# The first up-projection step of six feed-forward passes, made in token halves

## The chip, the cores and the metric

The kernel runs as one launch on one core of a Trainium2 chip. The metric is the device time of that launch in microseconds, the median of the runs. Five engines work side by side and meet only through semaphores: TensorE (PE, with its weight loads listed as PEld), VectorE (DVE), ScalarE (ACT), GpSimd (POOL) and SyncE (SP). Transfers run on DMA queues.

## The reference, cut to what matters

Two blocks follow each other over one sequence of 256 tokens with 1024 features, each block with two layers. Every layer has a feed-forward pass (hidden width 2816), a mix of three branches with gates, and a second feed-forward pass:

```python
def swiglu(x, w_in, w_out):
    a, b = jnp.split(x @ w_in, 2, axis=-1)
    return (jax.nn.silu(a) * b) @ w_out

# first block, each of 2 layers
x = x + 0.5 * swiglu(rmsnorm(x, ffn1_norm[l]), w_ffn1_in[l], w_ffn1_out[l])
...                                       # the mix
x = x + 0.5 * swiglu(rmsnorm(x, ffn2_norm[l]), w_ffn2_in[l], w_ffn2_out[l])
# second block, each of 2 layers
x = _layer_norm(DN_ALPHA * x + 0.5 * _swiglu(x, ffn1_w1[l], ffn1_w2[l]), ln1_g[l], ln1_b[l])
...                                       # the mix, and its layer norm
x = _layer_norm(DN_ALPHA * x + 0.5 * _swiglu(x, ffn2_w1[l], ffn2_w2[l]), ln3_g[l], ln3_b[l])
```

That makes eight feed-forward passes. All data are float32.

## The kernel before, in words

**Tiling.** Tokens are 2 tiles of 128 (`TT`), features 8 tiles of 128 (`KD`), the hidden width 22 tiles (`FT`). The residual stream `x` and its normalised copy `xn` lie with tokens on the partitions. A product wants features on the partitions, so PE transposes: `turn` (L403 to L412) makes four 128x128 transposes (the instruction is L410) into a PSUM bank `T0` or `T1`; `turn_x` (L414) does so for token tile 0, features 0 to 3 in `T0` and 4 to 7 in `T1`, and then the same for token tile 1. Each filled bank is then read twice: ACT rounds it into `xT_upper` (L1519, `uppers`), and DVE writes the remainder to `xT_rest` (L1010, `rests`) and so releases the bank.

**Products in two parts.** Weights and activations are each held as a float32r upper part and a float32r rest. `product` makes three matmuls for one product: upper by upper, upper by rest, rest by upper. All matmuls are recorded under L361.

**The stream of weights.** The weights come as pieces of 128x1024 float32, 220 for each layer. SP loads a piece into one of four places of `ring`; ACT rounds it into `upper` (L1519), POOL subtracts to `rest` (L896) and thereby empties the ring place, so that SP may load it again. `upper` and `rest` have four places too; a place is free when PE has made the last matmul on it, which `mm` signals with the next matmul that carries no other signal (`free()` puts the piece on a list, `state["free"]`). ACT and POOL work ahead of PE by at most four pieces.

**A feed-forward pass.** `ffn` (L480) makes for each hidden tile j an `up(j)` (L488) and, one tile behind, a `down(j - 1)` (L500). `up(j)` takes two pieces (v = 0, 1, the two halves of the first weight matrix) and fills one PSUM bank `A0` or `A1`: for each piece 8 feature tiles of 3 matmuls with 256 moving columns (both token tiles), 48 matmuls in all. ACT then makes the silu of the first half, DVE multiplies by the second and splits into `hT`. `down(j)` takes one piece: 4 output banks `Y0` to `Y3` of 3 matmuls with 512 columns.

**Order before a pass.** In six of the eight passes `turn_x` stands directly ahead of the pass: `ffn(0)` and `ffn(1)` of the first block and `ffn(1)` of the second, in two layers each. The pass starts with `wait_xT` (L421), which waits until DVE has read both banks of token tile 1. The two other passes (`ffn(0)` of the second block) find `xT` already turned. Every engine runs its own program in the order written; there is no planner at run time.

Of the kernel before, what the change touches and what calls it, by code (L numbers as in the profile page):

```python
# [23 lines left out]
ALL = slice(None)  # L24

P = 128
# [121 lines left out]
def emit(nc, a, book):  # L148
# [4 lines left out]
    with ExitStack() as ctx:  # L153
# [202 lines left out]
        def _(pe):  # L356
# [31 lines left out]
            def cut(parts, *index):  # L388
                return tuple(p[index] for p in parts)
# [21 lines left out]
                    at_col += P  # L411
                i.then_inc(*filled(label))  # L412

            def turn_x(src, label, ready):  # L414
                for tt in range(TT):
                    pe.wait_ge(*ready(tt))
                    for h in range(2):
                        turn(f"T{h}", label + (tt, h),
                             [src[:, tt, (4 * h + q) * P:(4 * h + q + 1) * P] for q in range(4)])

            def wait_xT(label):  # L421
                for h in range(2):
                    pe.wait_ge(*taken(label + (1, h)))
# [53 lines left out]
                            also(k, cut(s, ALL, q))  # L477
                    free()

            def ffn(f, xlabel):  # L480

                if xlabel is None:
                    for h in range(2):
                        pe.wait_ge(*sig[f"T{h} read"].value(0))
                else:
                    wait_xT(xlabel)

                def up(j):  # L488
                    lab = ("ab", f, j)
                    out = fill(pe, f"A{j % 2}", lab)  # L490
                    for v in range(2):
                        s = shaped(piece(), PIECE, "p (k c) -> p k c", k=KD)
                        for k in range(KD):
                            product(out[:, v * S:(v + 1) * S], cut(s, ALL, k), cut(xT, ALL, k),
                                    k == 0, k == KD - 1, filled(lab) if v == 1 and k == KD - 1 else None)
                        free()

                ys = []

                def down(j):  # L500
                    s = piece()
                    pe.wait_ge(*sig["hidden"].after((f, j)))
                    if j == 0:
                        ys.extend(fill(pe, f"Y{b}", ("y", f, b)) for b in range(4))
                    for t in range(TT):
                        for n in range(2):
                            product(ys[2 * t + n], cut(hT, ALL, j % 2, slice(t * P, (t + 1) * P)),
                                    cut(s, ALL, slice(n * 512, (n + 1) * 512)),
                                    j == 0, j == FT - 1, filled(("y", f, 2 * t + n)) if j == FT - 1 else None)
                    free()  # L510

                for j in range(FT):
                    up(j)
                    if j:
                        down(j - 1)
                down(FT - 1)
                state["A"] = 0
# [82 lines left out]
            with region(pe, BLOCK1):  # L600
                state["piece"] = 0
                assert not state["free"]
                turn_x(xn, ("norm", 0), lambda tt: sig["scaled"].after((0, tt)))
                ffn(0, ("norm", 0))

                pe.wait_ge(*sig["memory scaled"].after(0))
                by_features("mk", 2, rhs=(memTg,))
# [111 lines left out]
                          lambda h, kt: VX[:, kt, h * P:(h + 1) * P], P, False, between=turn_both)  # L719
                turn_o("mem", lambda qt: taken(("o", "mem", 0, qt)))  # L720
                merge()
                turn_x(xn, ("norm", 2), lambda tt: sig["scaled"].after((2, tt)))
                ffn(1, ("norm", 2))
                leave_last()

            with region(pe, BETWEEN):
# [15 lines left out]
            with region(pe, BLOCK2):  # L742
                state["piece"] = 0
                assert not state["free"]
                ffn(0, None)
                turn_x(x, ("norm", 0), lambda tt: sig["x normed"].after((0, tt)))
                wait_xT(("norm", 0))
                by_features("qa", 2)
# [82 lines left out]
                    free()  # L831
                turn_o("fox", lambda qt: taken(("o", "fox", 1, qt)))
                merge()
                turn_x(x, ("norm", 1), lambda tt: sig["x normed"].after((1, tt)))
                ffn(1, ("norm", 1))
                leave_last()
                turn_x(x, ("norm", 2), lambda tt: sig["x normed"].after((2, tt)))

# [1133 lines left out]
```

## Time and profile before

| | us |
|---|---|
| median of 3 runs | 3139.74 (3139.7 to 3140.13) |
| profiled execution, its own time | 3141.49 |
| span of that execution, first to last instruction | 3139.8 |
| PE busy | 2877.2 (92%) |
| POOL busy | 2067.8 (66%) |
| ACT busy | 1232.5 (39%) |
| DVE busy | 946.9 (30%) |
| mean granted TensorE clock | 0.950 of full |

Busy times are of one profiled execution. A matmul's record lasts longer than the step from its start to the next one's start, since matmuls overlap; what a run of n matmuls costs is read from starts, or as (length of the merged row, less one record) / (n - 1). The granted clock is 1.00 at 2.4 GHz and 0.50 at 1.2 GHz.

### The profile page before, as it was taken

Reading aid. Unit: us, or ns where it says so; the run is one execution under the profiler, and the core shown is the slowest. Engines: PE = TensorE matmul, PEld = TensorE weight load, DVE = VectorE, ACT = ScalarE, POOL = GpSimd, SP = SyncE. Lnnn points to the kernel's source line nnn. Section 1 sums busy time; section 2 is a strip of 40 time slices with the busy share of each in tenths; the row PEclk is TensorE's granted clock in tenths of the full one; section 3 lists DMA queues with packets and bytes.
Section 4 is the critical chain, followed back from the end, with each engine's and each line's share of the span. In section 5 each row is a group of like instructions: output and inputs, shape, how many; then the busy total and the mean of one; then the engine's idle time right before and its main releaser. Section 6 shows DMA issues by size and latency. Waiting matters only on the chain.

```text
span 3139.8 us, 55072 instructions
## 1 busy us (share of the span) xinstructions
PE 2877.2 (92%) x19786; PEld 2676.7 (85%) x19786; DVE 946.9 (30%) x1601; ACT 1232.5 (39%) x1522; POOL 2067.8 (66%) x905
## 2 busy tenths in 40 slices
PE   5999979899899988899899899888989989988898
PEld 4997778899798868889889899888989989988897
DVE  2111274311211146521111222752121122375212
ACT  3433434344442443344344343334443434333444
POOL 4875454788685734578768774347877867425787
PEclk8999989999899999999899998999999999999999
DMA  5555433555554532355545454235555544413554
GB/s 204 188 176 169 140 108 100 178 187 188 172 187 155 189 121 95 127 182 188 170 159 186 151 167 148 68 108 174 187 176 172 184 150 157 154 61 111 178 188 155
DMA packets 131939, 491.31 MB, mean 156 GB/s; under 512 B 14656, under 2 KB 14656, under 8 KB 129632
## 3 DMA queue, kind: packets, MB, share of 16 engines
q1 hardware_dynamic: 128256, 467.10, 45.3%
q0 software_dynamic: 3424, 20.71, 1.9%
q8 instruction: 167, 2.74, 0.4%
q14 instruction: 92, 0.75, 0.1%
HBM read 485.63 MB, written 2.13 MB: 155 GB/s over the span
## 4 chain that ended last, share of the span: by engine, by line
PE 38%; issue 27%; POOL 26%; DVE 6%; ACT 1%; POOLq 1%; DMA 0%; DVEq 0%; ACTq 0%; SPq 0%
POOL rest L896 26%; PE psA L361 23%; PE psY L361 13%; PE psT L410 2%; DVE st L1086 1%; ACT Sc L1519 1%; POOLq L893 1%; DVE xT_rest L1010 0%; DVE PT L1318 0%; ACT xT_upper L1519 0%; DVE Sc L1091 0%; DVE Sc L1081 0%; DVE xT_upper L1169 0%; DVE arena L1165 0%; DMA cst<-in_consts 0%
## 5 line engine op out<-in xcount | busy, mean ns | idle before, releaser
L896 POOL TENSOR_TENSOR rest<-ring,upper 128x1024 fp32r<-128x1024 f32 (+1 forms) x836 | 2025.8, 2429 | 919.6 <-ACT upper L1519 902.6
L1519 ACT ACTIVATE upper<-ring 128x1024 fp32r<-128x1024 f32 (+1 forms) x836 | 877.0, 1050 | 1048.3 <-PE psA L361 833.4
L361 PE MATMUL psA<-xT_upper,upper 128*128 128x256 f32 x3456 | 987.3, 286 | 16.8 <-DVE xT_rest L1010 12.7
L361 PE MATMUL psA<-xT_rest,upper 128*128 128x256 f32 x3456 | 985.8, 285 | 0.0
L361 PE MATMUL psA<-xT_upper,rest 128*128 128x256 f32 x3456 | 985.6, 285 | 0.0
L361 PEld LDWEIGHTS psA<-xT_upper,upper 128*128 128x128 f32 x3456 | 671.3, 194 | 28.0 <-issue 19.8
L361 PEld LDWEIGHTS psA<-xT_rest,upper 128*128 128x128 f32 x3456 | 671.2, 194 | 6.2
L361 PEld LDWEIGHTS psA<-xT_upper,rest 128*128 128x128 f32 x3456 | 670.9, 194 | 0.0
L1066 DVE TENSOR_TENSOR sil<-sil,psA 128x256 f32<-128x256 f32 x176 | 74.1, 421 | 1257.6 <-ACT sil L1519 1257.6
L361 PE MATMUL psY<-upper,hT_upper 128*128 128x512 f32 x704 | 276.0, 392 | 0.0
L361 PE MATMUL psY<-rest,hT_upper 128*128 128x512 f32 x704 | 275.9, 392 | 0.0
L361 PE MATMUL psY<-upper,hT_rest 128*128 128x512 f32 x704 | 273.9, 389 | 0.0
L361 PE MATMUL psY<-xT_upper,upper 128*128 128x256 f32 (+1 forms) x784 | 236.4, 302 | 6.4 <-POOL rest L896 6.3
L361 PE MATMUL psY<-xT_rest,upper 128*128 128x256 f32 (+1 forms) x784 | 228.4, 291 | 0.0
L361 PE MATMUL psY<-xT_upper,rest 128*128 128x256 f32 (+1 forms) x784 | 227.9, 291 | 0.0
L1519 ACT ACTIVATE sil<-psA 128x256 f32<-128x256 f32 x176 | 67.7, 385 | 295.6 <-PE psA L361 295.6
L361 PEld LDWEIGHTS psY<-xT_upper,upper 128*128 128x128 f32 (+1 forms) x784 | 155.9, 199 | 7.1 <-POOL rest L896 6.7
L361 PEld LDWEIGHTS psY<-xT_rest,upper 128*128 128x128 f32 (+1 forms) x784 | 156.1, 199 | 1.8
L361 PEld LDWEIGHTS psY<-upper,hT_rest 128*128 128x128 f32 x704 | 132.2, 188 | 28.9
L361 PEld LDWEIGHTS psY<-xT_upper,rest 128*128 128x128 f32 (+1 forms) x784 | 155.4, 198 | 0.5
L361 PEld LDWEIGHTS psY<-upper,hT_upper 128*128 128x128 f32 x704 | 132.9, 189 | 23.1
L361 PEld LDWEIGHTS psY<-rest,hT_upper 128*128 128x128 f32 x704 | 132.9, 189 | 21.1
(231 smaller groups left out, 3300.8 us busy)
## 6 DMA issues: line engine op xcount, KB each, us to landing
ring<-in_weights SPq DMA_DIRECT2D x884, 512.0 KB, 3.4
G<-in_rows POOLq DMA_DIRECT2D x13, 1024.0 KB, 5.1
OT<-memory_transposed POOLq DMA_DIRECT2D x2, 1024.0 KB, 5.2
G<-rel_by_distance POOLq DMA_DIRECT2D x1, 2048.0 KB, 9.7
G<-in_mem SPq DMA_DIRECT2D x1, 1024.0 KB, 5.1
x<-in_x SPq DMA_DIRECT2D x1, 1024.0 KB, 10.7
memory_transposed<-arena POOLq DMA_DIRECT2D x1, 1024.0 KB, 8.3
par<-in_params POOLq DMA_DIRECT2D x4, 256.0 KB, 3.6
```

The lines of the kernel that those rows point to most:

```text
L361: i = pe.matmul(out, lhsT, rhs, start=start, stop=stop)
L410: i = pe.transpose(out[0:t.shape[1], at_col:at_col + P], t, ident)
L893: pool.wait_ge(*free_)
L896: pool.tensor_tensor(rest[:, r, 0:n], ring[:, r, 0:n], upper[:, r, 0:n], ALU.subtract)\
L1066: tt_(v, v, at(lab)[:, S:2 * S], ALU.mult).then_inc(*read(lab))
L1086: link(dve.tensor_reduce(m, sc, AX, ALU.max))
L1519: act.activation(out, in_, func, **kw).then_inc(*up)
```

## The change

In the six passes with a turning directly ahead, the turning moves into `ffn`, and `up(0)` is replaced by `up_by_halves`: turn token tile 0, wait for its two banks, make all products of both pieces for token tile 0 (48 matmuls of 128 columns), then turn token tile 1, wait, and make the 48 matmuls of 128 columns for token tile 1. The first piece goes on the free list after its last product in the second half, the second piece after its own. `up(1)` and all that follows is as before, and the other engines' programs are unchanged.

```diff
-            def turn_x(src, label, ready):
-                for tt in range(TT):
+            def turn_x(src, label, ready, halves=range(TT)):
+                for tt in halves:
                     pe.wait_ge(*ready(tt))
...
+            def wait_half(label, tt):
+                for h in range(2):
+                    pe.wait_ge(*taken(label + (tt, h)))
+
+            def ffn(f, src=None, xlabel=None, ready=None):
...
+                def up_by_halves():
+                    lab = ("ab", f, 0)
+                    out = fill(pe, "A0", lab)
+                    parts = [shaped(piece(), PIECE, "p (k c) -> p k c", k=KD) for _ in range(2)]
+                    for tt in range(TT):
+                        turn_x(src, xlabel, ready, [tt])
+                        wait_half(xlabel, tt)
+                        for v in range(2):
+                            for k in range(KD):
+                                product(out[:, v * S + tt * P:v * S + (tt + 1) * P], cut(parts[v], ALL, k),
+                                        cut(xT, ALL, k, slice(tt * P, (tt + 1) * P)), k == 0, k == KD - 1,
+                                        filled(lab) if (tt, v) == (1, 1) and k == KD - 1 else None)
+                            if tt == 1:
+                                state["free"].append(state["piece"] - 2 + v)
...
                 for j in range(FT):
-                    up(j)
+                    if j == 0 and src is not None:
+                        up_by_halves()
+                    else:
+                        up(j)
...
-                turn_x(xn, ("norm", 0), lambda tt: sig["scaled"].after((0, tt)))
-                ffn(0, ("norm", 0))
+                ffn(0, xn, ("norm", 0), lambda tt: sig["scaled"].after((0, tt)))
...
-                turn_x(xn, ("norm", 2), lambda tt: sig["scaled"].after((2, tt)))
-                ffn(1, ("norm", 2))
+                ffn(1, xn, ("norm", 2), lambda tt: sig["scaled"].after((2, tt)))
...
-                turn_x(x, ("norm", 1), lambda tt: sig["x normed"].after((1, tt)))
-                ffn(1, ("norm", 1))
+                ffn(1, x, ("norm", 1), lambda tt: sig["x normed"].after((1, tt)))
```

## Rows read from the trace of the kernel before

**Rows 1.** The page, part 1: busy us, share of the span, instructions.

```profile
PE 2877.2 (92%) x19786; PEld 2676.7 (85%) x19786; DVE 946.9 (30%) x1601; ACT 1232.5 (39%) x1522; POOL 2067.8 (66%) x905
```

**Rows 2.** The page, part 5: busy us, mean ns, idle before, releaser.

```profile
L896 POOL TENSOR_TENSOR rest<-ring,upper 128x1024 fp32r<-128x1024 f32 (+1 forms) x836 | 2025.8, 2429 | 919.6 <-ACT upper L1519 902.6
...
L361 PE MATMUL psA<-xT_upper,upper 128*128 128x256 f32 x3456 | 987.3, 286 | 16.8 <-DVE xT_rest L1010 12.7
```

**Rows 3.** The waits of all engines: us in total, times, longest us.

```profile
ACT upper L1519 <- PE psA L361: 833.4, 463, 7.8
```

**Rows 4.** Windows, tile psT, six turnings (first, and all): us, busy (count), PEclk.

```profile
40.60:46.70 6.10, 3.93 (x16) 3.00 (x16) 2.77 (x4) 2.39 (x4) 0.50 0.81 273
...
sum 35.80, PE 21.85 PEld 16.86 DVE 16.41 ACT 14.11; mean PE 3.64 PEld 2.81 DVE 2.74 ACT 2.35
```

**Rows 5.** Windows, tile psA, six up(0) (first, last, and all), same columns.

```profile
46.70:54.01 7.31, 7.29 (x49) 7.29 (x50) 0.00 (x0) 0.00 (x0) 0.79 0.06 26
...
2935.65:2943.90 8.25, 8.23 (x50) 8.24 (x50) 0.00 (x0) 0.00 (x0) 0.68 0.66 238
sum 49.25, PE 49.12 PEld 49.16 DVE 0.00 ACT 0.00; mean PE 8.19 PEld 8.19 DVE 0.00 ACT 0.00
```

**Rows 6.** Timeline, third turning: start us, length us, engine, line, operands, count, idle.

```profile
796.09 1.97 PE L410 MATMUL psT<-cst,xn 128*128 128x128 f32 x8 [9.50 <-DVE xn L1018]
798.72 0.69 DVE L1010 TENSOR_TENSOR xT_rest<-psT,xT_upper 128x512 fp32r<-128x512 f32 x1 [0.16 <-ACT xT_upper L1519]
801.25 0.69 DVE L1010 TENSOR_TENSOR xT_rest<-psT,xT_upper 128x512 fp32r<-128x512 f32 x1 [0.16 <-ACT xT_upper L1519]
802.17 0.57 PE L361 MATMUL psA<-xT_upper,upper 128*128 128x256 f32 x1 [1.59 <-DVE xT_rest L1010]
```

**Rows 7.** Timeline of the second turning, its token tile 0.

```profile
591.10 1.09 PE L410 MATMUL psT<-cst,xn 128*128 128x128 f32 x8 [3.58 <-DVE xn L1018]
592.42 1.29 DVE L1010 TENSOR_TENSOR xT_rest<-psT,xT_upper 128x512 fp32r<-128x512 f32 x2 [0.26 <-ACT xT_upper L1519]
```

**Rows 8.** Timeline of PE at the high clock, 512 and 256 columns in sequence.

```profile
613.25 0.39 PE L361 MATMUL psY<-rest,hT_upper 128*128 128x512 f32 x1
...
613.70 0.28 PE L361 MATMUL psA<-xT_upper,upper 128*128 128x256 f32 x1
613.82 0.28 PE L361 MATMUL psA<-xT_rest,upper 128*128 128x256 f32 x1
```

**Rows 9.** Timeline of PE, runs of narrow plain float32 matmuls.

```profile
440.68 1.95 PE L361 MATMUL psA<-PT 128*128 128x128 f32 x16
...
1558.76 9.53 PE L361 MATMUL psA<-Sc 32*128 32x8 f32 x44
...
1893.30 1.87 PE L361 MATMUL psA<-Sc,ring 128*128 128x30 f32 x16
```

**Rows 10.** Windows around two PE pauses, and two runs of narrow matmuls.

```profile
1083.00:1091.00 8.00, 6.02 (x29) 5.02 (x28) 1.92 (x2) 2.86 (x4) 5.22 (x3) 0.79 0.46 145
2649.00:2657.00 8.00, 6.41 (x42) 5.72 (x42) 1.38 (x2) 2.12 (x2) 5.55 (x3) 1.00 0.61 207
...
1559.00:1568.00 9.00, 9.00 (x44) 9.00 (x44) 0.00 (x0) 0.00 (x0) 1.63 (x2) 0.50 0.55 178
1893.00:1897.00 4.00, 4.00 (x36) 4.00 (x36) 0.00 (x0) 2.31 (x5) 1.79 (x2) 1.00 0.58 204
```

**Rows 11.** Groups by shape: the plain float32 matmuls of 256 columns.

```profile
L361 PE MATMUL psA<-OT,ring 128*128 128x256 f32 x128 | 27.9, 379 | 0.0
```

**Rows 12.** Timeline of ACT, second pass: splits of pieces, the first silu.

```profile
595.66 1.05 ACT L1519 ACTIVATE upper<-ring 128x1024 fp32r<-128x1024 f32 x1
...
602.53 1.06 ACT L1519 ACTIVATE upper<-ring 128x1024 fp32r<-128x1024 f32 x1 [4.06 <-PE psA L361]
603.61 1.28 ACT L1519 ACT_TABLE_LOAD   x1
605.40 0.38 ACT L1519 ACTIVATE sil<-psA 128x256 f32<-128x256 f32 x1 [0.51 <-PE psA L361]
```

More of the change, by code:

```diff
@@ L478, in by_tokens @@
                     free()
-            def ffn(f, xlabel):
-                if xlabel is None:
+            def wait_half(label, tt):
+                for h in range(2):
+                    pe.wait_ge(*taken(label + (tt, h)))
+            def ffn(f, src=None, xlabel=None, ready=None):
+                if src is None:
                     for h in range(2):
                         pe.wait_ge(*sig[f"T{h} read"].value(0))
-                else:
-                    wait_xT(xlabel)
+                def up_by_halves():
[12 more added lines that the diff above has]
+                                state["free"].append(state["piece"] - 2 + v)
                 def up(j):
@@ L744, in _ @@
                 assert not state["free"]
-                ffn(0, None)
+                ffn(0)
                 turn_x(x, ("norm", 0), lambda tt: sig["x normed"].after((0, tt)))
```

## The prediction

> **What bounds the kernel now.** I read the page's busy times first: PE is busy 92% of the span, no other engine over 66% [rows 1]. The costliest groups show what it does: up-projection matmuls of 256 columns in three like groups of 3456, with almost no idle time before them [rows 2]. The waits say who waits for whom: ACT, the engine that splits the weight pieces, stood 833 us until PE had released a piece [rows 3]. So in a feed-forward pass the splitting follows PE, and a microsecond that PE loses there is a microsecond of the kernel: the engines behind can't run ahead by more than their four places, and there is nothing later in the pass that waits for anything but PE.
>
> The windows over the six turnings and over the six first steps `up(0)` come next, since only these change. The turnings last 35.8 us together, 5.97 each [rows 4], the 48 matmuls behind them 49.25 us, 8.21 each [rows 5]; together 14.18 us for a pass, from the first transpose to `up(1)`. The reader is to see the clock: 48 matmuls at the full clock would be 48 x 0.12 = 5.8 us [rows 8]. They take 8.2, since the turning leaves PE at the low clock, and it stays there for a part of them. From the granted clock of the first and the last window (0.79 and 0.68 [rows 5]), 2 x 0.21 x 7.31 = 3.1 and 5.3 us of these were at 1.2 GHz. The mean of the six: 8.21 less 5.76 and less 0.15 for the slow first matmul leaves 2.3 us of excess; a matmul at the low clock takes 0.213 us (below), so 2.3 / (1 - 0.12 / 0.213) = 5.3 us.
>
> **The change part by part, for one pass.**
>
> *The start comes sooner.* Before, the first product waits for the remainders of both token tiles. In the third turning PE's first transpose starts at 796.09, the second remainder of token tile 0 ends at 798.72 + 0.69 = 799.41, that of token tile 1 at 801.25 + 0.69 = 801.94, and the product follows at 802.17, 0.23 later [rows 6]. After the change it follows the first of these ends: 799.41 + 0.23 - 796.09 = 3.55 us after the first transpose, 2.5 us sooner. Four of the six turnings look like this one; two (the second and fourth, before `ffn(1)` of the first block) have a token tile 0 turned at the high clock: 592.42 + 1.29 + 0.23 - 591.10 = 2.84 us [rows 7]. Mean (4 x 3.55 + 2 x 2.84) / 6 = 3.31 us.
>
> *The second turning has nothing beside it.* It used to start while DVE was still busy with token tile 0. Now PE has issued all of half 0 when it starts, and the 48 products of half 1 are queued behind its wait, `up(1)` behind these; nothing else is ready for PE. It costs the whole chain of transposes, ACT's copy, DVE's subtraction: 2.84 us if the clock is high by then, 3.55 if not. I take 2.84. So the two turnings cost 3.31 + 2.84 = 6.15 us instead of 5.97: the sooner start is given back whole, and 0.2 us on top. The second waits for `xn` or `x` of token tile 1 cost nothing, these are long written.
>
> *The products double in number.* 48 matmuls of 256 columns become 96 of 128, each with its own weight load. What a 128-column float32r matmul costs no row shows. At the high clock 256 columns go in 0.12 us and 512 in (613.70 - 613.25) / 2 = 0.225 [rows 8], that is columns / 2.4 GHz and 0.013 us. By columns alone the narrow one would take 0.053 + 0.013 = 0.067 us. But narrow plain float32 matmuls with 128-column weight loads don't get there: 16 with 30 columns last 1.87 us, less one record of 0.27 over 15 steps 0.107 us each, and 16 with 128 columns (1.95 - 0.28) / 15 = 0.111 [rows 9]. Thirty columns can't need 0.107 us; the weight load sets this pace. At the low clock it is (9.53 - 0.36) / 43 = 0.213 us even with 8 columns [rows 9], the same as for 256 columns (256 / 1.2 GHz). From above, if a narrow float32r product cost what a product in plain float32 does (below), it is 0.222. I take 0.115, between the nearest row (0.111) and the 0.12 that the 256-column one needs: 96 x 0.115 = 11.04 us instead of 5.76.
>
> The Trainium skill (TensorE: Matmul & The Clock Gate, LDWEIGHTS) gives a weight load as its columns / 1.2 GHz, an estimate of 0.107 us for 128; the trace agrees. The same page (Back-to-back issue gap) gives a pair of weight load and 128-column matmul as about 81 ns; by that the 96 would be 7.8 us and the kernel an estimated 19 us below my forecast (6 x 3.2). No row here shows a pair with a full weight load under 0.107, which is why I don't take it.
>
> *The clock.* With 5.3 us at the low clock again, the excess is 5.3 x (1 - 0.115 / 0.213) = 2.44 us (before: 5.3 x (1 - 0.12 / 0.213) = 2.31), and 0.15 us as before for the first matmul. The new pause in the middle is one of 1.8 us idle behind 1.1 us of transposes; A pause of 8.00 - 6.41 = 1.6 us between products left the clock at 1.00 in one stretch, one of 2.0 us threw it to the low level in another (0.79 over the window) [rows 10]. Ours is of that size, so I count a fall in two of the six passes, 2.4 us each (again 5.3 us at the low clock), that is 0.8 us a pass; in all six it would be 2.4 and 0.7 more where the second turning is slow too. If the sooner start lifts the clock 2.5 us sooner, 1.1 us is won.
>
> *Releases.* Piece 0 is released after three quarters of the step instead of half, 24 x 0.115 = 2.8 us before `up(1)`; piece 1 at its end as before. In the passes `ffn(1)` ACT must still split pieces 2 and 3, which stand behind its last copy of the turning (595.66, right behind it [rows 12]): ACT 1.05 each, POOL 2.43 each [rows 2], so piece 2 is ready 2.7 us and piece 3 some 5.1 us after half 1 starts; `up(1)` wants them at 5.5 and 8.4. Piece 4, released at 2.8, split by ACT until 3.9 and by POOL by 7.5 (8.1 where POOL first issues a load of rows), is wanted at 11.3. The first silu follows a split and a 1.28 us table load [rows 12]: ready at 5.2, just ahead of the 5.5 at which the bank is full. All of it stays hidden, with 2.5 us to spare; without that cover the most is one split, 2.4 us. SP's loads follow POOL's splits as before. POOL's load of rows in the second block waits some 10 us longer for the turning; it is used only behind the pass. On DVE, the scaling of `x` or of the memory (under 4 us) moves behind half 1's remainders and ends before the silu.
>
> **Sum.** After: 3.31 + 2.84 + 11.04 + 2.44 + 0.15 + 0.8 = 20.58 us; before 14.18; plus 6.4 us for a pass, 38.4 us for six. The profiled execution takes 3141.49 us, its span 3139.8 and 1.7 outside; it becomes 3179.9. The median of the runs is 1.75 us below the profiled one, so the forecast is 3139.74 + 38.4 = 3178 us. Its own range: a pause that never throws the clock back (-5), the clock sooner (-6) and a pace of 0.107 (-4) give 3163; a pause that always does (+14) and a pace of 0.12 (+3) give 3195.
>
> **Rivals.**
>
> *Narrow float32r goes at the price of plain float32.* The trace shows float32r at one column a cycle only from 256 columns up. A plain float32 product is recorded as two matmuls, each at two cycles a column: 27.9 us / 128 = 0.218 us for 256 columns [rows 11], and 0.111 for 128 [rows 9], so 0.222 for a product. At that, 96 x 0.222 = 21.3 us; the low clock 5.3 x (1 - 0.222 / 0.427) = 2.5; a pass 3.31 + 2.84 + 21.3 + 2.5 + 0.15 = 30.1, plus 15.9, kernel 3139.74 + 96 = 3235 us (3225 to 3250). For it: nothing excludes it. Against it: float32r goes as one pass at 256 and at 512 columns [rows 8], and one record stands for each part. 0.27.
>
> *The clock stays low.* A narrow product streams columns for only half of its time. 44 matmuls of 8 columns in a row left the clock at 0.50 for 9 us [rows 10]. Against it: at 30 columns, between gate products, it stayed at 1.00 [rows 10], and 128 is far from 8. All 96 at 0.213: 3.31 + 3.55 + 20.45 + 0.15 = 27.5, plus 13.3, kernel 3139.74 + 80 = 3220 us; with only half 1 or parts of it low, 3195 to 3220. 0.15.
>
> *Not slower: the columns set the pace.* If float32r loads hide behind one another better than plain ones do, a narrow product takes 0.067 us (low clock 0.107, half 0 wholly in it). Then 3.31 + 2.84 + 6.43 + 1.9 + 0.15 = 14.6, plus 0.45, kernel 3142 us. It decides for no measurable change from a pace of about 0.073 us down; the sooner start can't bring more, because the second turning eats it, and piece 2 (ready after 2.7 us) would then be wanted at 3.2. Against it: 0.107 with 30 columns [rows 9]. 0.06.
>
> **Chances.** Forecast 0.50, plain price 0.27, clock low 0.15, columns set the pace 0.06, other 0.02. What a measurement of this kernel tells from no change is about 0.2%, 6 us. Slower by more: 0.93; within: 0.05; faster: 0.02. The range goes from the forecast's lower end, 3163, through the clock case and the better part of the plain price, to 3244; outside lie the third rival, the top of the first, and tails.
>
> **What would show it.** Right: 576 instead of 288 matmul records in the six steps, all of 128 columns and one record for each of the three parts, at 0.11 to 0.12 us from start to start at the high clock; the first at 0.23 us behind the second remainder of token tile 0; a PE pause of about 1.8 us behind the second eight transposes; no ACT or POOL split as releaser of PE in `up(1)`. Wrong: a pace of 0.067 or 0.22, more records than that, a granted clock of 0.50 through half 1, or a feed-forward step later in the pass that got longer.

## The result and the profile after

The changed kernel takes 3234.85 us (median of 4 runs, 3229.8 to 3237.57), against 3139.93 for the kernel before in the same comparison (4 runs, 3139.7 to 3153.28). The ratio is 1.028 with the interval [1.0264, 1.0297], so it is slower by some 95 us. The profiled execution took 3236.47 us with a span of 3234.8, 95.0 us more than the profiled execution before.

The page's first part (busy us, share of the span, instructions) answers to [rows 1]:

```profile
PE 2971.7 (92%) x20074; PEld 2771.4 (86%) x20074; DVE 947.3 (29%) x1601; ACT 1232.9 (38%) x1522; POOL 2067.2 (64%) x905
```

PE has 288 instructions more, as the code says, and 94.5 us more of busy time; the other engines' busy times moved by less than 1 us. The groups by shape (busy us, mean ns | idle before and releaser) answer to [rows 2]; the second line is one of three like groups and new:

```profile
L361 PE MATMUL psA<-xT_upper,upper 128*128 128x256 f32 x3360 | 958.2, 285 | 6.8 <-DVE xT_rest L1027 3.2 <-issue 2.8 <-POOL rest L913 0.8
...
L361 PE MATMUL psA<-xT_upper,upper 128*128 128x128 f32 x192 | 80.4, 419 | 17.3 <-DVE xT_rest L1027 17.3
```

A record of half the columns lasts 419 ns where one of 256 columns lasts 285. Three groups of 192 are 576 records, one for each part of each product, so float32r still goes in one pass; what is long is something else. The timeline of the second pass (start us, length us) shows it from start to start:

```profile
606.39 1.09 PE L410 MATMUL psT<-cst,xn 128*128 128x128 f32 x8 [3.57 <-DVE xn L1035]
609.05 0.47 PE L361 MATMUL psA<-xT_upper,upper 128*128 128x128 f32 x1 [1.57 <-DVE xT_rest L1027]
...
618.92 0.41 PE L361 MATMUL psA<-xT_rest,upper 128*128 128x128 f32 x1
619.14 0.41 PE L361 MATMUL psA<-xT_upper,rest 128*128 128x128 f32 x1
619.35 1.93 PE L410 MATMUL psT<-cst,xn 128*128 128x128 f32 x8
622.69 0.47 PE L361 MATMUL psA<-xT_upper,upper 128*128 128x128 f32 x1 [1.41 <-DVE xT_rest L1027]
```

From 609.05 to 619.14 there are 47 steps: 0.215 us each, and 0.213 (619.35 less 619.14 is 0.21) once they run. That is the pace of the low clock in [rows 9] (0.213 us), not the 0.111 of the high one. The first eight transposes still took 1.09 us, the second eight 1.93. Windows on the product bank, from the first narrow product to `up(1)`, for all six passes (us, PE busy, PEld busy, DVE, ACT, then the granted clock) answer to [rows 5], whose sum was 49.25:

```profile
42.18:66.12 23.94, 20.80 (x96) 20.61 (x97) 0.00 (x0) 0.00 (x0) 1.00 0.10 39
609.05:632.99 23.94, 20.80 (x97) 20.61 (x97) 0.00 (x0) 0.00 (x0) 0.50 0.25 88
827.34:851.27 23.93, 20.79 (x96) 20.60 (x97) 0.00 (x0) 0.00 (x0) 0.50 0.10 39
1394.08:1418.02 23.94, 20.80 (x96) 20.61 (x97) 0.00 (x0) 0.00 (x0) 0.50 0.26 88
...
sum 143.63, PE 124.79 PEld 123.67 DVE 0.00 ACT 0.00; mean PE 20.80 PEld 20.61 DVE 0.00 ACT 0.00
```

All six are alike to 0.01 us. The clock stands at 0.50 for the whole of 24 us in five of them. The first reads 1.00, but its 96 matmuls take the same 20.80 us, so the clock's record is missing there and the pace tells: low too. The turnings, as windows on the transposes' banks up to the first product of each half, answer to [rows 4] (sum there 35.80; here the third turning, both its parts, the first part of the second, and the sum of all twelve):

```profile
606.39:609.05 2.66, 1.09 (x8) 0.85 (x8) 1.29 (x2) 1.08 (x2) 0.76 0.02 6
...
823.96:827.34 3.38, 1.96 (x8) 1.56 (x8) 1.38 (x2) 1.19 (x2) 0.50 0.66 264
837.64:840.98 3.34, 1.92 (x8) 1.52 (x8) 1.38 (x2) 1.19 (x2) 0.50 0.00 0
...
sum 38.88, PE 21.59 PEld 17.11 DVE 16.41 ACT 14.11; mean PE 1.80 PEld 1.43 DVE 1.37 ACT 1.18
```

**Where the 95.0 us are.** The first halves of the turnings are 2 x 2.66, 3 x 3.38 and 3.37, together 18.83 us; with the 143.63 of the windows above, 162.46 us lie between the first transpose and `up(1)`, where 85.05 lay before: +77.4. The clock does not rise at `up(1)` at once either. The window behind the second pass shows it at 0.79 over 5 us:

```profile
633.00:638.00 5.00, 5.00 (x35) 5.00 (x36) 0.42 (x1) 0.38 (x1) 0.79 0.32 108
```

From the first transpose to the first work of the next stage the six passes grew by 15.13, 12.58, 14.10, 12.92, 14.13 and 15.13 us, together 84.0; so this tail costs 84.0 - 77.4 = 6.6. The other 11 us lie in stages whose instructions the change leaves alone, above all in the two mixes of the second block. One of them as whole windows, before and after:

```profile
1776.00:2147.00 371.00, 338.63 (x2444) 321.30 (x2444) 167.43 (x246) 139.10 (x187) 189.52 (x80) 0.94 0.38 127
```

```profile
1832.00:2209.00 377.00, 343.76 (x2444) 326.36 (x2444) 167.68 (x246) 139.12 (x187) 190.00 (x80) 0.92 0.37 125
```

The same 2444 matmuls, the same work on DVE, ACT and POOL, 5.1 us more of PE's busy time and a clock of 0.92 in place of 0.94. The second block's other mix, the same work again, grew from 373.5 to 377.3 us. How much of this the change causes isn't shown: in the profiled executions of E1 and E2 below, where these stages hold the same instructions, one of them lasts 369.5 us in E1 and 381.2 in E2, so they differ from execution to execution by more than the 9.8 us in question. The kernel before, too, came to medians of 3141.7 to 3146.8 us in the comparisons below, 2 to 7 us above the 3139.93 here.

### The profile page after: what moved, and what is told of

It reads as the page before. It is cut to its first block, busy times and chain, and to the rows that moved or that the text cites. A ratio compares the mean times of both kernels' runs of the same rounds, so it can differ in the third digit from the quotient of the medians.

```text
span 3234.8 us, 55660 instructions
## 1 busy us (share of the span) xinstructions
PE 2971.7 (92%) x20074; PEld 2771.4 (86%) x20074; DVE 947.3 (29%) x1601; ACT 1232.9 (38%) x1522; POOL 2067.2 (64%) x905
## 4 chain that ended last, share of the span: by engine, by line
PE 41%; POOL 25%; issue 25%; DVE 7%; ACT 1%; POOLq 1%; DMA 0%; DVEq 0%; SPq 0%; ACTq 0%
PE psA L361 27%; POOL rest L913 25%; PE psY L361 12%; PE psT L410 2%; DVE st L1103 1%; ACT Sc L1536 1%; POOLq L910 1%; DVE xT_rest L1027 1%; DVE Sc L1098 0%; DVE PT L1335 0%; ACT xT_upper L1536 0%; DVE Sc L1108 0%; DVE xT_upper L1186 0%; DVE arena L1182 0%; DMA cst<-in_consts 0%
## 5 line engine op out<-in xcount | busy, mean ns | idle before, releaser
L361 PE MATMUL psA<-xT_upper,upper 128*128 128x256 f32 (+1 forms) x3552 | 1038.6, 292 | 24.0 <-DVE xT_rest L1027 20.5
L361 PE MATMUL psA<-xT_rest,upper 128*128 128x256 f32 (+1 forms) x3552 | 1036.5, 292 | 0.0
L361 PE MATMUL psA<-xT_upper,rest 128*128 128x256 f32 (+1 forms) x3552 | 1036.3, 292 | 0.0
L361 PEld LDWEIGHTS psA<-xT_upper,upper 128*128 128x128 f32 x3552 | 714.8, 201 | 37.3 <-DVE xT_rest L1027 21.7
L361 PEld LDWEIGHTS psA<-xT_rest,upper 128*128 128x128 f32 x3552 | 715.1, 201 | 6.2
L361 PEld LDWEIGHTS psA<-xT_upper,rest 128*128 128x128 f32 x3552 | 714.6, 201 | 0.0
## 6 DMA issues: line engine op xcount, KB each, us to landing
x<-in_x SPq DMA_DIRECT2D x1, 1024.0 KB, 10.7
```

The source lines that it names most:

```text
L361: i = pe.matmul(out, lhsT, rhs, start=start, stop=stop)
```

## The experiments

The accounts to be told apart were these. The first: a stream of narrow float32r products doesn't lift a low clock, and the turning leaves it low; the pause between the halves is then innocent. The second: the pause in the middle throws the clock down. The third: narrow products are slow by themselves, whatever the clock. Ratios are to the kernel before on the same chip, with their 95% intervals.

**E1: both token tiles turned first, then the 96 narrow products without a pause.** Edit to the changed kernel:

```diff
+                    turn_x(src, xlabel, ready)
                     for tt in range(TT):
-                        turn_x(src, xlabel, ready, [tt])
                         wait_half(xlabel, tt)
```

> The changed kernel, but both token tiles are turned before the first product; half 0 waits only for its own two banks. No pause stands between the halves any more. Theory A (a stream of 128-column float32r products does not lift TensorE's clock): granted clock 0.50 and 0.213 us a product through all 96, which then take 20.4 us; the first product comes about 4.5 us after the first transpose, so a pass from first transpose to up(1) is 25 us against 14.2 before, and with the low clock lasting a little into up(1) the kernel takes about 3210 us. Theory B (the second turning and its pause keep the clock low): the clock rises some 5 us into the 96, a pass is about 18 us, the kernel about 3163 us.

Measured: 3208.48 us (4 runs, 3190.49 to 3218.46), ratio 1.0196 [1.0145, 1.0247]. Windows over the first and the second pass:

```profile
43.00:53.50 10.50, 10.50 (x97) 10.50 (x96) 3.92 (x6) 3.11 (x5) 1.01 (x1) 1.00 0.18 75
594.50:615.00 20.50, 20.50 (x98) 20.50 (x97) 1.38 (x2) 4.99 (x6) 7.03 (x3) 0.50 0.26 97
```

Without any pause between them 96 products ran at the low clock from end to end, in five passes of six. In the first pass the clock had risen before the first product, and the same 96 took 10.5 us at the high one. So the pause isn't needed for the loss, and in this run the stream kept whichever clock it started with. The time is the 3210 us of the first account, not the 3163 of the second.

**E2: the same 96 narrow products, but in `up(10)`, in the middle of all eight passes.** Edit to the kernel before:

```diff
                     out = fill(pe, f"A{j % 2}", lab)
+                    if j == 10:
+                        parts = [shaped(piece(), PIECE, "p (k c) -> p k c", k=KD) for _ in range(2)]
+                        for tt in range(TT):
+                            for v in range(2):
+                                for k in range(KD):
+                                    product(out[:, v * S + tt * P:v * S + (tt + 1) * P], cut(parts[v], ALL, k),
+                                            cut(xT, ALL, k, slice(tt * P, (tt + 1) * P)), k == 0, k == KD - 1,
...
```

> The kernel before, with only the up-projection of hidden tile 10 of all eight feed-forward passes made as 96 products of 128 columns; they start in the middle of a stream at the high clock, with no turning near. It measures the price of a narrow float32r product at the high clock. Theory A1 (weight load sets the pace, clock holds): 0.11 to 0.12 us each at granted clock 1.00, 5.3 us more a pass, kernel about 3182 us. Theory A2 (narrow products also make the clock fall): 0.115 first, then 0.213 at granted clock 0.50; up to 14.7 us a pass and some us at the low clock behind it, kernel 3220 to 3270 us. Theory C (a narrow float32r product costs what a plain float32 one does): 0.21 to 0.22 each from the first on at granted clock 1.00, kernel about 3260 us.

Measured: 3190.26 us (4 runs, 3174.49 to 3192.99), ratio 1.0127 [1.0088, 1.0167]. The window around one such step, and the group by shape:

```profile
686.00:698.00 12.00, 12.00 (x103) 11.79 (x102) 0.00 (x0) 2.53 (x4) 6.26 (x3) 1.00 0.40 133
```

```profile
L361 PE MATMUL psA<-xT_upper,upper 128*128 128x128 f32 x256 | 70.0, 273 | 0.0
```

95 steps took 10.55 us, 0.111 each, in all eight passes, and the clock stayed at 1.00. The record is 273 ns where that of the changed kernel is 419, for the same instruction. This is the pace that narrow products have at 2.4 GHz, and it refutes the third account and with it the price of plain float32: 8 x (96 x 0.111 - 48 x 0.12) = 39 us, near the 45 measured (28 to 52 by the interval).

**E3: the same number of matmuls in `up(0)`, but wide.** Edit to the kernel before: `up(0)` of the six passes makes each of its 48 products of 256 columns twice, the second time over the first.

```diff
+                    if j == 0 and xlabel is not None:
...
+                        for again in range(2):
+                            for v in range(2):
+                                for k in range(KD):
+                                    product(out[:, v * S:(v + 1) * S], cut(parts[v], ALL, k), cut(xT, ALL, k),
+                                            k == 0, k == KD - 1,
...
```

> The kernel before, with the 48 products of up(0) made twice over in the six passes (96 products of 256 columns, 96 weight loads, same wait for both tiles). It keeps the number of the changed kernel and gives back the width. Theory A (width decides on the clock): the clock rises about 5 us in as before, the other products take 0.12 us; plus 48 x 0.12 = 5.8 us a pass, kernel about 3174 us. Rival (the number of products and weight loads right behind the turning keeps the clock low): 0.213 us through all 96, plus about 12 us a pass, kernel about 3215 us.

Measured: 3180.02 us (4 runs, 3174.9 to 3186.91), ratio 1.0114 [1.0085, 1.0144]. The second pass in two windows:

```profile
599.60:605.60 6.00, 5.95 (x28) 5.96 (x29) 0.00 (x0) 1.06 (x1) 4.70 (x2) 0.50 0.33 109
605.60:611.20 5.60, 5.60 (x48) 5.60 (x48) 0.00 (x0) 0.00 (x0) 0.00 (x0) 1.00 0.25 88
```

The clock rose 13 to 27 matmuls in (14 to 28 in the kernel before), in the first pass it was high from the start, and the added 48 cost 0.12 each: 6 x 48 x 0.12 = 34.6 us, measured 35.1. At the low clock wide and narrow matmuls start 0.213 us apart alike; the wide stream was followed by a rise in each of the five passes that began low, the narrow one of E1 in none of its five.

**E4: PE kept at work while the norm and the turning run.** Edit to the kernel before: unneeded matmuls (plain float32, 256 columns, constants into the free bank `A1`) ahead of and behind the six turnings, 20, 7 or 13 ahead and 3 behind.

```diff
+            def keep_busy(n):
...
+                for _ in range(n):
+                    pe.matmul(BANK["A1"][:, 0:S], ident, CM, start=True, stop=True)
...
+                keep_busy(7)
                 turn_x(xn, ("norm", 2), lambda tt: sig["scaled"].after((2, tt)))
+                keep_busy(3)
                 ffn(1, ("norm", 2))
```

> The kernel before, with plain float32 matmuls of 256 columns on constants into the unused bank A1 while PE waits for the norm (20, 7 or 13 matmuls ahead of the six turnings, by the length of the wait) and 3 behind each turning. If the low clock behind the turning is what costs: the first products of up(0) go at 0.12 us, 2.3 us saved a pass and 0.7 for the transposes in four, kernel about 3123 us. Rival (the clock falls within the turning anyway, or the extra matmuls end late): no gain, 3140 to 3150 us.

Measured: 3138.5 us (10 runs, 3131.29 to 3143.11), ratio 0.9977 [0.9963, 0.999]. The timeline of PE in the second pass and the window behind it:

```profile
585.90 3.18 PE L427 MATMUL psA<-cst 128*128 128x256 f32 x14
589.64 1.09 PE L410 MATMUL psT<-cst,xn 128*128 128x128 f32 x8 [0.55 <-DVE xn L1032]
591.70 1.26 PE L410 MATMUL psT<-cst,xn 128*128 128x128 f32 x8 [0.97 <-DVE xT_rest L1024]
592.79 1.46 PE L427 MATMUL psA<-cst 128*128 128x256 f32 x6
594.54 0.38 PE L361 MATMUL psA<-xT_upper,upper 128*128 128x256 f32 x1 [0.29 <-DVE xT_rest L1024]
```

```profile
594.60:600.40 5.80, 5.80 (x49) 5.80 (x50) 0.00 (x0) 3.40 (x3) 5.78 (x3) 1.00 0.39 131
```

The 48 products of `up(0)` take 5.8 us at the full clock in every pass; `up(1)` starts 10.7 to 10.8 us after the first transpose in five passes and 12.2 in the first, instead of 13.3 to 14.6, together 18.6 us sooner. The kernel gained only 7, and the 3123 us expected were missed. A part of the answer is in the two passes of the second block:

```profile
2145.41 11.82 POOL L910 TENSOR_TENSOR rest<-ring,upper 128x1024 fp32r<-128x1024 f32 x5
```

```profile
2151.26 6.12 DVE L1082 CAST hT_upper<-sil 128x256 fp32r<-128x256 f32 x1
```

```profile
2158.26 0.49 PE L361 MATMUL psY<-upper,hT_upper 128*128 128x512 f32 x1 [2.15 <-DVE hT_rest L1083]
```

POOL waits for the last remainder of the turning, loads rows, and then makes five splits without a break, 2.4 us each, until 2157.23. DVE's rounding of the first hidden tile, a CAST that takes 0.29 us elsewhere, begins beside them, lasts 6.12 us and ends at 2157.38, 0.15 behind the last split. PE's `down(0)` waits for this CAST and the subtraction behind it and starts 18.84 us after the first transpose, where it does at 16.5 in the second to the fourth pass. The pieces themselves came in time: `down(0)` takes the third of the five, split by about 2152.5 (11.82 / 5 us each). The last pass is the same (6.12 us), so this takes back 4.7 us. Of the 176 CASTs of this kind in each of the thirteen profiled executions, no others last over 0.5 us. Another 7.4 us of the profiled execution are the two mixes of the second block again (374.9 and 377.0 us, before 371.0 and 373.5), and what of that is chance isn't shown.

**E5: the changed kernel, with PE kept at work ahead of the first turning.** As many unneeded matmuls as in E4, 20, 7 and 13; nothing between the halves.

```diff
                 merge()
+                keep_busy(7)
                 ffn(1, xn, ("norm", 2), lambda tt: sig["scaled"].after((2, tt)))
```

> The changed kernel with extra matmuls on constants ahead of the six passes (20, 7 or 13 of 256 columns, in PE's wait for the norm), nothing between the halves. Theory A (narrow float32r products hold the clock that they meet, high or low): half 0 runs at 0.111 us a product, the pause of the second turning is too short to matter, half 1 as well; a pass is 2.8 + 5.3 + 2.8 + 5.3 = 16.3 us from first transpose to up(1), 2.1 more than before and about 11 less than in the changed kernel: some 0.4% slower than before, about 3155 us. Theory B (the second turning throws the clock down even so, and half 1 then can't lift it): half 0 at 0.111, half 1 at 0.213 and a few us behind it low, 9 us a pass above before, about 3195 us.

Measured: 3219.19 us (4 runs, 3216.68 to 3235.36), ratio 1.0253 [1.0224, 1.0282]. The third pass in four windows:

```profile
829.00:835.20 6.20, 5.47 (x49) 5.47 (x50) 0.68 (x2) 0.00 (x0) 0.20 (x1) 1.00 0.50 172
835.20:838.00 2.80, 1.23 (x11) 0.99 (x11) 1.52 (x4) 1.09 (x2) 0.00 (x0) 1.00 0.00 0
838.00:841.40 3.40, 3.40 (x25) 3.40 (x24) 2.40 (x2) 0.21 (x1) 0.00 (x0) 0.74 0.00 0
841.40:846.40 5.00, 5.00 (x25) 5.00 (x25) 0.00 (x0) 2.34 (x2) 2.35 (x1) 0.50 0.00 0
```

Half 0 ran high, all 48 in 5.5 us; then came the second turning with its pause, and the clock fell some 2 us into half 1 and stayed down. Two passes went like this. In three others it fell already within half 0 (27 to 43 of its products slow) and half 1 was low altogether; the first pass was low. So the time lies above both of the times expected. A high clock throughout would have given back 6 x 96 x (0.213 - 0.111) = 59 us; by the medians 16 came, by the ratios 8, and the two intervals overlap. What made the clock fall, E5 alone doesn't tell: each fall came some 0.5 to 2 us into narrow products behind a pause of about 1.5 us. In E2 no pause stands ahead of the narrow products, in the later passes of E11 none longer than 1.0 us, and in their profiled executions the clock held; so the pauses of the turnings are the likelier cause, which is argued and not shown. Once down, it stayed down through the rest of the narrow products.

**E6 and E7: the splits moved ahead.** E6 is E4 with pieces 2 and 3 of `ffn(1)` split before the turning on ACT and POOL, and the unneeded matmuls may carry the release of a piece (`mm`); E7 is E6 with unneeded matmuls at the other turnings as well.

```diff
-                    pe.matmul(BANK["A1"][:, 0:S], ident, CM, start=True, stop=True)
+                    mm(BANK["A1"][:, 0:S], ident, CM, True, True)
...
                 norm_power(2)
+                until(AFTER_MIX)
                 pool.wait_ge(*sig["scaled"].after((2, 1)))
```

```diff
                 ffn(0, None)
+                keep_busy(16)
                 turn_x(x, ("norm", 0), lambda tt: sig["x normed"].after((0, tt)))
+                keep_busy(3)
                 wait_xT(("norm", 0))
```

> The kernel before with the matmuls on constants of e4_keep_busy, and with the splits of pieces 2 and 3 of each ffn(1) moved ahead of the turning on ACT and POOL (their places are released one step sooner, since the extra matmuls carry the releases). In e4 a pass gained 3.3 us until up(1), but in the second block up(1) and the first down then ended 2.5 to 3 us later than they should, with POOL splitting without a break. If that wait ate the gain: about 2 x 3 us more than e4, ratio to before about 0.994. If the loss lies elsewhere (the clock in the attention stages): as e4, 0.997 to 0.998.

> e6_busy_splits with extra matmuls also around the turnings of the mix (norm 1 of the first block, norm 0 of the second) and the last norm of the second block's layers, all of which start their products at the low clock for 13 to 28 of the first matmuls. 2 to 3 us in each of six places at most if the clock is what they wait for: ratio to before about 0.990. If not: as e6.

Measured: E6 3143.02 us (12 runs, 3137.44 to 3151.39), ratio 0.9996 [0.9985, 1.0007]; E7 3133.61 us (11 runs, 3129.01 to 3145.15), ratio 0.9964 [0.9952, 0.9975]. E6 gave E4's gain back by the ratio, where 0.994 was expected, and E7 missed its 0.990. E6's timeline, where the norm's scaling meets POOL's subtraction:

```profile
586.40 4.57 DVE L1034 SCALAR_TENSOR_TENSOR xn<-x,st,G 128x1024 f32<-128x1024 f32 x2
...
586.95 6.23 POOL L910 TENSOR_TENSOR rest<-ring,upper 128x1024 fp32r<-128x1024 f32 x2
```

The pair of scalings takes 4.57 us beside POOL, and in the four passes of `ffn(1)` the first product comes 7.1 to 7.8 us after the first transpose instead of 4.9. The splits, moved ahead, stand beside the very scaling that PE waits for.

**E8 and E9: the splits moved to behind the scaling.** E8 is E6 with POOL's splits after DVE's scaling of both token tiles and still ahead of its load of rows (the diff is to E4); E9 is E8 with E7's further unneeded matmuls.

```diff
                 pool.wait_ge(*sig["scaled"].after((2, 1)))
+                until(AFTER_MIX)
                 load_rows(l * 3 + 3)
...
                 norm_power(1)
+                pool.wait_ge(*sig["x normed"].after((1, 1)))
+                until(AFTER_MIX)
```

> e6_busy_splits with one thing changed: POOL makes the splits of pieces 2 and 3 only after DVE has written the normalised rows. In e6 DVE's two scalar_tensor_tensor of 1024 columns took 4.57 us instead of 2.48, one of them 3.36 instead of 1.28, while POOL subtracted beside them, and the first product came 7.2 us after the first transpose instead of 4.9. Theory (the two engines slow each other): DVE back at 1.28 us each, first product at 4.9 to 5.1 us, 2.3 us a pass in four passes won back against e6 and the late pieces of e4 gone as well; ratio to before about 0.995. If the first product stays at 7 us, ACT's earlier splits are what delays the turning.

> e7_busy_all with the same one change: 9 us less than e7, ratio to before about 0.993; with the rival (ACT's splits delay the turning) as e7, 0.996.

Measured: E8 3128.48 us (6 runs, 3125.74 to 3130.63), ratio 0.994 [0.992, 0.996]; E9 3125.12 us (6 runs, 3119.21 to 3128.02), ratio 0.9926 [0.9906, 0.9947]. The same scaling in E8:

```profile
588.41 2.48 DVE L1035 SCALAR_TENSOR_TENSOR xn<-x,st,G 128x1024 f32<-128x1024 f32 x2
```

2.48 us for the pair and the first product at 4.9 us in five passes (6.4 in the first). ACT's splits are as early as in E6, so it was POOL's that made the scaling long. The slow CAST of E4 is gone as well: `up(2)` starts at 19.2 to 19.3 us in these five, where E4 had 21.7 in two of them. E8 has the 19 us that E4 should have had. Of the 10 us by which its median lies below E4's, the CAST explains 4.7; in the profiled executions another 4.0 are one of the mixes (370.9 us for 374.9). E9 has the lowest median of this study, though its runs overlap with E8's; both beat the kernel before and the changed one.

**E10: narrow plain float32 in place of the wide ones.** E4 without matmuls ahead of the turning, and behind it 24 unneeded matmuls of 128 columns (48 records).

```diff
-                keep_busy(7)
                 turn_x(xn, ("norm", 2), lambda tt: sig["scaled"].after((2, tt)))
-                keep_busy(3)
+                keep_busy(24)
...
-                    pe.matmul(BANK["A1"][:, 0:S], ident, CM, start=True, stop=True)
+                    pe.matmul(BANK["A1"][:, 0:P], ident, CM[:, 0:P], start=True, stop=True)
```

> The kernel before, with 24 plain float32 matmuls of 128 columns on constants (48 records) behind each of the six turnings, none ahead. They meet the low clock as the changed kernel's half 0 does and have the same 128 columns and the same weight loads, but each record streams its columns at two cycles a column, so the array has columns for all of the time. Theory A (the share of time with columns decides whether the clock comes back): it rises some 5 us into them, and up(0) then goes at 0.12 us throughout; about 3.4 us a pass more, kernel about 3165 us. Rival (matmuls of 128 columns don't lift it, whatever they stream): 0.213 us through all 48 and up(0) as before, 8.2 us a pass more, kernel about 3193 us.

Measured: 3156.26 us (10 runs, 3149.33 to 3162.15), ratio 1.0029 [1.0013, 1.0044]. The third pass:

```profile
802.22 6.70 PE L427 MATMUL psA<-cst 128*128 128x128 f32 x48
...
808.88 0.28 PE L361 MATMUL psA<-xT_rest,upper 128*128 128x256 f32 x1
```

```profile
802.00:807.00 5.00, 5.00 (x35) 5.00 (x35) 4.01 (x6) 1.01 (x3) 0.00 (x0) 0.73 0.34 139
807.00:809.00 2.00, 2.00 (x21) 2.00 (x19) 0.00 (x0) 0.00 (x0) 0.00 (x0) 1.00 0.04 8
```

The clock rose 12 records into the 48 here and held through the rest and through `up(0)`; in four other passes it rose 2 to 10 records in, and in one just before the first of them, when PE had only made the transposes, which are plain float32 of 128 columns too. So 128 columns as such don't keep the clock low: with plain float32 of that width the clock was up 2.5 us into these records at the latest, in all six passes, and 20.3 us of float32r of that width in E1 didn't raise it. What sets the two apart for the clock isn't shown. The time is 9 us above the kernel before, less than either account expected (25 and 53).

**E11: E1 with PE kept at work ahead of the turning.** Then both turnings follow, and the 96 narrow products without a pause.

```diff
                 merge()
+                keep_busy(7)
                 ffn(1, xn, ("norm", 2), lambda tt: sig["scaled"].after((2, tt)))
```

> e1_turn_first (both tiles turned first, half 0 waits for its own banks only, 96 narrow products) with the matmuls on constants of e5 ahead of the turning: the token halves at their best, with no second pause and a high clock. If the clock is high when the narrow products begin, they hold it: first product 3.2 us after the first transpose, 96 x 0.111 = 10.7 us, up(1) at 13.9 us, against 14.2 in the kernel before and 10.8 in e4: kernel about as before, ratio 0.998 to 1.002. If the clock falls in the turning, they can't lift it: 0.213 us for what is left of them, up to 10 us a pass more, ratio up to 1.019.

Measured: 3162.92 us (6 runs, 3144.49 to 3169.04), ratio 1.0075 [1.0049, 1.01]. The second pass of the profiled execution:

```profile
594.20:605.00 10.80, 10.80 (x99) 10.80 (x98) 1.29 (x2) 5.09 (x6) 5.82 (x3) 1.00 0.54 196
```

The same 96 products behind the same turning as in E1, whose window read 0.50, and now 0.111 each in all five later passes, only because PE came to the turning from work. From the first transpose to `up(1)` it is 13.8 us in these five (15.0 in the first), no more than before the change and some 3 more than in E4: the products cost 96 x 0.111 - 48 x 0.12 = 4.9 us more, and the first of them comes 3.0 to 3.1 us after the first transpose instead of 4.9, since it needs token tile 0 alone. Only the profiled execution (3144.49 us) is within the expected ratio of 0.998 to 1.002; it was the fastest of the six, and the whole interval lies above. The others had a mean clock of 0.954 to 0.959 against 0.962, so the clock was probably lost in some passes there, which no trace shows.

## Why the prediction was wrong

The direction was right (0.93 on slower) and the time was inside the range, which reached that far for two rivals and not for the forecast; +38 us were forecast and +95 measured. Step by step, for one pass:

**The sooner start: right.** Forecast 3.31 us, measured 18.83 / 6 = 3.14. The first product starts 0.05 us behind the second remainder (609.05 against 607.71 + 1.29), where I had taken 0.23.

**The second turning has nothing beside it: right, and mis-sized.** Forecast 2.84, measured 3.34 in all six, because the clock was low by then; the pause is 1.41 us of idle behind 1.93 us of transposes, not 1.8 behind 1.1.

**The pace of a narrow product: right.** Forecast 0.115 at the high clock; E2, E1's first pass and E11 show 0.111, the low edge of what the rows of plain float32 allowed [rows 9]. One record stands for each part. At either clock the pace hardly depends on the columns (0.107 us with 30 and 0.111 with 128, 0.213 with 8 as with 128), so the weight load, which all of these have alike, is what I take to set it; no run here changes its size.

The Trainium skill (TensorE: Matmul & The Clock Gate, LDWEIGHTS) gives a load as its columns / 1.2 GHz, 0.107 us for 128, with no second figure for the low clock. E2's 0.111 for load and matmul together agrees; at the low clock the same pair takes 0.213 in the changed kernel. The same page of the Trainium skill (Back-to-back issue gap) has about 81 ns for such a pair, which no run here met.

**The clock: this is the step that failed.** I carried over "with 5.3 us at the low clock again" from the wide products, as if the rise were a matter of time. It then counted 2.44 us, and 0.8 for a fall in two passes of six, 14.43 us with the pace and the first matmul for all products. Measured are (143.63 - 6 x 3.34) / 6 = 20.60 us: 96 products at the low clock from first to last, 6.2 us a pass more. The clock fell before them, in two passes within the first turning (0.76 and 0.77 over it) and in the others earlier (in [rows 5] it was low at this place too), and nothing that followed raised it until `up(1)`. With -0.17 for the start and +0.50 for the second turning that is 27.1 us in place of 20.58, or +39 us for six passes. The rest of the gap of 56.6 us is what I hadn't counted at all: the rise delayed into `up(1)`, 6.6 us, and the phases of the clock elsewhere, 11.

The trace had said it in one row. The window 1559:1568 [rows 10] shows 44 narrow matmuls in an unbroken run that left the clock at 0.50. I put it aside with 30 columns at 1.00, but that row stands behind work at the high clock: it shows that a narrow stream can keep a high clock, not that it raises a low one. The two rows don't contradict each other, and the turning puts this kernel in the first of the two cases.

The same page of the Trainium skill (Part 1: The HAM clock gate) says that what is issued early in a run of work goes at the low clock and everything after it at the high one, and that this is a budget of time and not a number of matmuls. By that rule the forecast's step was sound. E1 is at odds with it: PE has no gap for 20.5 us and stays at 0.50. E3 agrees with it, with wide matmuls at the same spacing of starts.

**Releases: right.** Of PE's idle time before the up-projection matmuls, 0.8 us in the whole kernel was ended by a split of POOL. PE was slower here than forecast, which left the splits more time; the profiled execution of E11 runs near the forecast's pace, and there the 48 products of `up(1)` take 5.8 us in the five later passes, without a wait. What I had not seen is that POOL's splits can hold up DVE (E4).

**The rivals.** "The clock stays low" (0.15) described the mechanism: 27.5 us a pass, measured 27.1; its 3220 us lacks the 6.6 and the 11 and so fell 15 short. "The price of plain float32" (0.27) came out at 3235 us, which is the measured time, and is refuted all the same: one record a part, and 0.111 at the high clock and 0.213 at the low instead of 0.222 and 0.427. That the number fits is chance. "The columns set the pace" is refuted by the same 0.111.

## What to carry to other kernels

Before cutting a matmul's moving columns, look at what the clock is at that place: a stream of 128-column float32r matmuls kept a high clock in E2 and in E11's profiled execution, lost it behind a pause in E5, and didn't raise a low one (E1), so behind a pause the price of halving can be 2 x 0.213 against 0.12 and not 2 x 0.111. Splitting a step to shorten the wait ahead of it pays only if the second wait has work beside it; here it gave back 3.34 us for 2.8 gained (35.8 / 6 less 3.14). The gain at such a place lies in the clock: unneeded wide matmuls during the wait were worth some 3 us a pass, once POOL's splits no longer stood beside DVE's work that PE waits for (E8: 0.6%; E9, with further turnings: 0.7%).

## What the runs showed of the hardware

**Two engines in each other's way.** DVE's scaling (SCALAR_TENSOR_TENSOR, 128x1024 float32) has a mean of 1280 ns in E4 and 1279 in E8, and 1628 in E6, where POOL subtracts beside it. The group in E8 and in E6:

```profile
L1035 DVE SCALAR_TENSOR_TENSOR xn<-x,st,G 128x1024 f32<-128x1024 f32 x12 | 14.9, 1279 | 11.9 <-POOL st L886 11.6
```

```profile
L1034 DVE SCALAR_TENSOR_TENSOR xn<-x,st,G 128x1024 f32<-128x1024 f32 x12 | 19.1, 1628 | 11.4 <-POOL st L886 11.1
```

The affected pair goes from 2.48 to 4.57 us, and POOL's two subtractions beside it from 2.4 us each to 3.1. The stronger case is the CAST of E4: 6.12 us for 0.29, ended 0.15 us behind the last of POOL's splits, though two of them had ended meanwhile. The Trainium skill (SBUF — State Buffer, Who interferes with whom) says that only DVE and GpSimd contend, by an exclusive lock. The CAST agrees with that. For the scalings it fits nearly: from the start of the first to the end of POOL's second subtraction it is 6.8 us (586.40 to 593.18), where one behind the other would take 2.48 + 2 x 2.4 = 7.3.

**The clock under a narrow stream can depend on what it was before.** The same 96 products behind the same turning ran at 0.111 us in one pass and at 0.213 in the next of one execution (E1), and whichever it was lasted to the last of them. In E5 a high clock was lost on the way.

**A granted clock in the records can be wrong.** In the first pass of the changed kernel it reads 1.00 while 96 products take 20.80 us. The pace from start to start is the surer witness.
